# First experts of a two-block model: tokens scattered to their slots in DRAM instead of a one-hot dispatch on TensorE

## What is computed

```python
def grouped_experts(x, expert, gate, w_gate, w_up, w_down):
    # tokens sorted by expert, each expert's rows padded to whole chunks
    xs = jnp.concatenate([x, jnp.zeros((1, d), x.dtype)], axis=0)[slot_tok].reshape(n_blocks, DISPATCH_BLOCK, d)
    ...
    def run(args):
        xb, e = args
        return (jax.nn.silu(xb @ w_gate[e]) * (xb @ w_up[e])) @ w_down[e]

    ys = lax.map(run, (xs, block_e)).reshape(cap, d)
    return jnp.zeros((n + 1, d), x.dtype).at[slot_tok].add(ys * slot_w[:, None])[:n]
```

## Time and profile before

| | |
|---|---|
| median of 3 runs | 2183.39 us (2183.11 to 2185.64) |
| profiled execution | 2182.89 us, its span 2181.1 us |
| busy in the span | TensorE 86%, weight loads 61%, DVE 41%, ACT 30%, GpSimd 25% |
| moved by DMA | 574.35 MB, 263 GB/s over the span |
| experts of layer 0 | 48 chunks, 366 to 897 us |
| experts of layer 1 | 37 chunks, 1173 to 1632 us |

### The profile page before, as it was taken

The page is one execution under the profiler, slowest core; times in us unless marked ns, Lnnn a source line. Parts: engine busy times, 40 slices in busy tenths (PEclk is TensorE's granted clock), DMA queues, the critical chain, the costliest instruction groups (busy, mean ns, idle before and its releaser), DMA issues.

```text
span 2181.1 us, 56144 instructions
## 1 busy us (share of the span) xinstructions
PE 1882.8 (86%) x23126; PEld 1338.9 (61%) x23127; DVE 896.6 (41%) x2096; ACT 656.3 (30%) x1229; POOL 551.5 (25%) x407
## 2 busy tenths in 40 slices
PE   5999989979977999699977997666666988899998
PEld 3555457657655667364566765545545775678886
DVE  2087243545543555644624442222224993310001
ACT  1100243534532454521533442222224322120001
POOL 0000002656644666200102442222239001000000
PEclk9999999999988999799998998888887997899999
DMA  9778648999999886532024999999993352133320
GB/s 374 288 273 306 231 177 338 422 424 422 421 423 421 363 324 257 186 116 82 26 78 171 400 425 421 420 424 422 420 416 132 116 193 77 39 116 135 135 97 20
DMA packets 133060, 574.35 MB, mean 263 GB/s; under 512 B 4720, under 2 KB 9840, under 8 KB 116464
## 3 DMA queue, kind: packets, MB, share of 16 engines
q1 hardware_dynamic: 132688, 570.72, 66.2%
q10 hardware_dynamic: 288, 2.43, 0.3%
HBM read 572.08 MB, written 1.05 MB: 263 GB/s over the span
## 4 chain that ended last, share of the span: by engine, by line
PE 62%; DMA 23%; DVE 6%; ACT 4%; issue 3%; SPq 1%; DVEq 0%; ACTq 0%
PE bank L325 24%; DMA ring<-in_expert_w_gate 15%; PE bank L511 15%; DMA ring<-in_expert_w_up 6%; PE bank L467 5%; PE bank L488 4%; PE bank L854 3%; PE bank L558 2%; DVE b L894 2%; ACT b L1573 2%; PE bank L396 1%; PE bank L777 1%; DMA ring<-in_conv_w_in 1%; SPq L2014 1%; DMA ring<-in_ada_w 1%
## 5 line engine op out<-in xcount | busy, mean ns | idle before, releaser
L511 PE MATMUL bank<-ring,b 128*32 128x128 f32 (+1 forms) x13600 | 538.1, 313 | 150.3 <-issue 66.7
L511 PEld LDWEIGHTS bank<-ring,b 128*32 128x32 f32 x13600 | 413.2, 117 | 333.0 <-issue 222.6
L894 DVE TENSOR_TENSOR h_t<-h_t,bank 128x512 f32<-128x512 f32 (+1 forms) x696 | 350.7, 566 | 560.9 <-PE bank L488 560.9
L1573 ACT ACTIVATE b<-bank 128x128 f32<-128x128 f32 (+3 forms) x546 | 186.2, 366 | 1155.1 <-PE bank L467 411.8
L325 PE MATMUL bank<-h_t,ring 128*128 128x256 f32 (+1 forms) x1728 | 470.0, 433 | 8.6 <-DVE h_t L1359 3.6
L325 PEld LDWEIGHTS bank<-h_t,ring 128*128 128x128 f32 x1728 | 333.0, 194 | 131.6 <-issue 91.1
L1962 POOL TENSOR_SCALAR b<-b 128x1024 f32<-128x1024 f32 (+1 forms) x85 | 195.3, 2297 | 79.3 <-POOL b L1970 37.1
L1970 POOL TENSOR_TENSOR b<-b 128x512 f32<-128x512 f32 (+1 forms) x85 | 89.7, 1056 | 476.4 <-PE bank L488 476.4
L1573 ACT ACTIVATE b<-b 128x256 f32 (+5 forms) x186 | 181.7, 1021 | 27.9 <-DVE b L894 14.5
L488 PE MATMUL bank<-b 32*128 32x512 f32 (+1 forms) x1392 | 176.8, 580 | 5.5 <-DVE h_t L894 4.8
L1965 POOL TENSOR_TENSOR b<-b,b 128x1024 f32<-128x1024 f32 (+1 forms) x85 | 161.1, 1895 | 7.1
(11 more groups left out here) (238 smaller groups left out, 1461.5 us busy)
## 6 DMA issues: line engine op xcount, KB each, us to landing
ring<-in_expert_w_gate SPq DMA_DIRECT2D x64, 2048.0 KB, 22.3
ring<-in_expert_w_up SPq DMA_DIRECT2D x64, 2048.0 KB, 24.3
ring<-in_expert_w_down SPq DMA_DIRECT2D x64, 2048.0 KB, 25.6
ring<-in_ada_w SPq DMA_DIRECT2D x24, 2048.0 KB, 18.8
ring<-in_w_mod SPq DMA_DIRECT2D x12, 2048.0 KB, 13.7
ring<-in_w_in SPq DMA_DIRECT2D x6, 2048.0 KB, 12.0
ring<-in_conv_w_in SPq DMA_DIRECT2D x5, 2048.0 KB, 20.1
ring<-in_w_ffn_gate SPq DMA_DIRECT2D x5, 2048.0 KB, 7.7
```

The lines of the kernel that those rows point to most:

```text
L511: last = pe.matmul(b[32 * m:32 * m + 32, 0:width], lhs[:, k, :], rhs[:, k, m * width:(m + 1) * width], start=(k == 0), stop=(k == nk - 1), ...
L894: return dv.tensor_tensor(o, a, b, op)
L1573: return ac.activation(o, i, f, **kw)
```

## The change

The experts of layer 0 get their tokens by DMA (`by_dma`), those of layer 1 as before.

- A tensor `slot_rows` in DRAM has a row of 1024 channels for each slot, 2176 in all. ACT issues one DMA behind its part of the first modulation that fills it with zeros, from a zeroed stretch of SBUF. DVE waits for `zeroed` before the router.
- DVE casts the slot numbers to integers (`slot_i`). After `placed` GpSimd issues eight indirect DMAs, for four tiles of 128 tokens and both slots of a token, each of which writes 128 rows of 4 KB to their slots. Its four diagonals come behind them.
- ACT waits for all eight (`scattered`) and loads the 32 rows of chunk 0 as 128 rows of 256 channels (`load_rows`, 128 KB). TensorE turns them with two transposes (`turn_rows`), ACT copies them to `xe` (`take_rows`) and issues the next chunk's load. In the loop the transposes stand where the dispatch stood, and turn the rows of chunk n+1.
- Gone in layer 0: the one-hot table, all dispatches, `take_quarter`, `take_xe`, `take_h`.
- In both layers the channels of `h_tok` are put in another order, with ACT's copies writing with a stride of 128. The dispatches ahead of layer 1's loop then read contiguous weights, and so does its `take_h`.
- TensorE counts the chunks in a register of its own (`chunk_no`).

```diff
+ROWS = P * (-(-(MOST + 2) * CAP // P))
...
+        slot_rows = nc.dram_tensor("slot_rows", (ROWS, D), F32).ap()
+        quarter_rows = slot_rows.rearrange("s (m c) -> (s m) c", m=4)
+        zeros = b3[:, 4736:5248]
...
+                def turn_rows(b):
+                    transposes(b, [(P * i, x_rows[:, P * i:P * i + P]) for i in range(2)]).then_inc(s["xq_full"], 1)
+
+                if by_dma:
+                    pass
+                else:
+                    pe.wait_ge(s["disp_ready"], 8)
+                    for q in range(4):
+                        dispatch(bank[q], lambda t, kk: h_tok[:, t, (2 * q + kk) * P:(2 * q + kk + 1) * P], 0)
...
-                pe.wait_ge(s["xq_taken"], 4)
+                if by_dma:
+                    pe.wait_ge(sem("rows_loaded"), 16)
+                    turn_rows(bank[3])
+                else:
+                    pe.wait_ge(s["xq_taken"], 4)
...
+                            if by_dma:
+                                pe.wait_ge(sem("rows_loaded"), n * 16 + 32)
+                                turn_rows(bank[3])
...
+                if layer == 0:
+                    for j in range(2):
+                        step(dv.tensor_copy(slot_i[:, 4 * j:4 * j + 4], fl(g[j])))
+                    done()
...
+            dv.wait_ge(sem("zeroed"), 16)
             moe(0, 4)
...
-                    taken(act(h_tok[:, t, cols], b[:, :], ACT.Copy))
+                    rows = h_tok[:, t, :].rearrange("p (k q) -> p q k", k=KD)
+                    taken(act(rows[:, 64 * half:64 * half + 64, :], b.rearrange("p (q k) -> p q k", k=KD), ACT.Copy))
...
+                def load_rows(n):
+                    ac.dma_start(x_rows, quarter_rows[bass.ds(n * P, P), :]).then_inc(sem("rows_loaded"), 16)
+
+                def take_rows(n):
+                    ac.wait_ge(s["xq_full"], n + 1)
+                    act(xe.rearrange("p (m h) s -> p h s m", h=2), bank[3][:, 0:256].rearrange("p (h s m) -> p h s m", h=2, m=4),
+                        ACT.Copy).then_inc(s["xe_taken"], 1)
+                    load_rows(n + 1)
...
+                if by_dma:
+                    ac.wait_ge(sem("scattered"), 16 * 8)
+                    load_rows(0)
...
             modulate(0, 0, "h_a0")
+            ac.dma_start(slot_rows.rearrange("(p r) (h c) -> p (r h) c", p=P, c=512),
+                         zeros.unsqueeze(1).broadcast_to([P, 2 * ROWS // P, 512])).then_inc(sem("zeroed"), 16)
...
                 po.wait_ge(sem(f"placed{layer}"), 1)
+                if layer == 0:
+                    for t in range(tiles):
+                        for j in range(2):
+                            at = bass.IndirectOffsetOnAxis(slot_i[:, 4 * j + t:4 * j + t + 1], 0)
+                            po.indirect_dma_start(slot_rows, at, h_tok[:, t, :], None).then_inc(sem("scattered"), 16)
```

## The result

The changed kernel takes 2217.7 us (median of 4 runs, 2216.6 to 2220.8), the kernel before 2184.0 (2183.1 to 2185.6): ratio 1.016, 95% interval 1.014 to 1.017. The profiled execution has a span of 2215.2 us, 34.1 more than before. I forecast slower by 12, to at most 2217; the sign holds, the size doesn't.

The account below looks back on a forecast made before the run. Bounds by stage: TensorE work counts in 17 of 48 first expert chunks, added bytes in the other stages. Profiled 2182.9 us plus 14 + 4 + 11 - 13.6 - 3 = +12.4 gives 2195.3, said as 2196; range 2181 to 2217.

Parts of the forecast that it names:

- Fill, +14: Opening: the zero fill shares the full DMA engines with queued weights, so the second convolution chunk comes late; +14 us.
- Rival A: Opening: the fill is hidden, since writes to DRAM don't compete with loads; 2182, no change; chance 0.17 shared with another rival.
- Entry, +4: Before layer 0's experts: scatter and row load replace the dispatch, and the stretch bound by loads starts at 382.5; +4 us.
- the next weight load is issued by then: Entry: prefetch and first row load end some 382.5, with the next weight load already issued, so no idle DMAs.
- The 15.5 us of dispatch: Entry: removing the one-hot table and 64 dispatch matmuls gains nothing; first gate at 366 to 371, where 366.36 was.
- Row loads, +11: DMA-bound stretch of layer 0's experts: each of 30 chunks pays 0.37 us for its row load; +11 us.
- the 25th expert's weights: Sign in layer 0's expert loop: these weights come some 15 us later.
- Compute-bound chunks, -13.6: Last 17 chunks of layer 0: transposes replace dispatch instructions and save 0.8 us a chunk; -13.6 us.
- The wait for `hid`: Last 17 chunks: TensorE waits for DVE's `hid` before the hidden transpose, so 0.8 us a chunk is gained, not 1.5.
- Rival C: Last 17 chunks: rows come late and TensorE waits; 2226, or 2210 for half of that; chance 0.23.
- Layer 1, -3: Before the second experts: contiguous dispatch weights give -4, strided token copies ahead of the router cost +1; -3 us.

Follow-up runs that it names:

- e1: The changed kernel with the zero fill issued in `gated`, at its second channel block, and no longer in the opening: 2208.6 us.
- e5: The kernel before with the new channel order of the token rows alone, no fill, scatter or row loads: 2178.5 us, ratio 0.9971.
- e2: The changed kernel with SyncE waiting for the scatter before it issues the six prefetched expert weights: 2204.4 us.
- e3: The changed kernel with SyncE's wait for the scatter in front of the fourth of the six prefetched weights: 2212.2 us.
- e11: The changed kernel with SyncE holding the six prefetched weights until the first row load has landed: 2206.3 us.
- e6: The changed kernel with ACT copying landed rows into a second tile, from which TensorE turns them, packets unchanged: 2213.9 us.

## Why the prediction was wrong

**Fill, +14: right in kind, 11.7 measured.** One packet for one packet, as said, ACT not held. The convolution chunk came 10.3 late, and the matmuls behind it took 8.71 for 7.03, as the term had it from the earlier trace rows. The term was 2 us too high because the chunk was there at 90.4 and not at 92.5: both queues together moved 408 GB/s, not 386. That the start came out right was luck: the fill was issued at 40.62, not at 44.6, but its first packet stood at 44.8. e1's profiled execution gives the term back in full. Rival A falls.

**Entry, +4: the step that failed; 23.2 measured, outside its bounds.** The prediction had the rule, packets in turn, and the three sizes, and still took the scatter to be done at 352 to 362. It let the scatter run beside the 2 KB packets of the last piece. In the trace its first packet is at 356, 4.6 us behind the first issue, and only 41 of the 2 KB packets start after that; from there it stood against the 16 KB packets of gates and ups, and in between against the 4 KB packets of the first down. By the prediction's own rule the time was to be had: the scatter has 64 packets an engine; 32 of them pass beside the 32 of two gates and two ups, at 0.16 + 0.61 us, and 32 beside those of the first down, at 0.32, which is 24.6 + 10.2 = 34.8 us. It took from 356 to 392.4. Its first issue was 17 us later than the diagonals in the earlier trace rows, of which the fill is 11.7 and the copies most of the rest. Then the second half of the step fell too: it held that the engines would not idle because "the next weight load is issued by then". But the first gate, which frees the slot, stood behind scatter and row load, and the engines idled for 16 us (21 at a share of 0.23). The 15.5 us of dispatch were not gained, as the prediction had said, since scatter and row load took their place; in the kernel before they did count, for e5, with a shorter dispatch, has its first gate 3.65 us earlier and its span 4.0 shorter. e2 and e3 show the cause. By the profiled spans e2 gives back 12.5 of the 23.2, and e11, with both waits cured, no more. The 10.7 that stay are not taken apart by any run here: the scatter's 4.2 MB are 10 us at 420 GB/s wherever they stand, and the entry also begins later by the copies.

The Trainium skill (DMA: Bandwidth & Descriptors, Queues, rings and completion order) has the turn by packets, and the trace agrees, with 187 to 184. The estimate worked out from the same page of the Trainium skill (Anatomy of one DMA), eight scatters one behind the other in 25.6 us, does not hold: in e2 the eight were issued from 352.5 on, 1.26 apart, and all there at 368.6.

**Row loads, +11: right, 11.1.** The prediction proposed to read it at the 25th expert's weights, some 15 late where the entry alone makes 4. They are 46.0 late, 34.9 of it from ahead of the loop.

**Compute-bound chunks, -13.6: -11.4 measured.** The wait for `hid` is there, 0.50 us before the transpose, in 11 of 17. The 0.8 was near: with rows in time a chunk takes 8.99 (e6), 0.9 less than the 9.89 before. Rival C came in part: rows late in 7 chunks, 4 us. In these chunks a row load took 6.0 us in the median, less than the 6.8 that I had worked out for a window of 7.7, but anything from 2.0 to 10.0; one figure for all of them hid the late ones. (In the stretch bound by loads the median is 9.2.)

**Layer 1, -3: -0.7.** The dispatch took 5.72 and not 3.9. The row, 0.12 us a matmul, was taken at full clock; here, behind waits for VectorE of 5 us and more, the granted clock was 0.67 in the mean of 1199 to 1205 us, so for the greater part at the lower of its two levels, 1.2 GHz. With strided weights this could not be seen: a matmul took 0.24 at a mean clock of 0.89 in layer 0 and 0.25 at 0.62 in layer 1. At full clock, in layer 0 of e5, the gain is 8.1 us for 64. And the copies took 1.6 more, not 1, all of it in front of the router.

The sum of the terms as measured, 11.7 + 23.2 + 11.1 - 11.4 - 0.7, is 33.9; 19 of the 21.5 us by which I missed lie in the entry.

## To carry over

Before a small-packet transfer is put on a critical path, count its packets an engine and multiply by the packet time of whatever else is queued there then: its bytes alone don't tell. 4 MB that took 12 us with the weights held back (e2) took 36 beside their 16 KB and 4 KB packets. A prefetch that is early for its own consumer should be held back behind such a transfer, and bulk writes belong where the window of DMA shares has a gap. When a change has several parts, time each alone: the one that was meant as a by-product, kept alone, is faster than both kernels.

## What the runs showed of the hardware

- A load of 128 x 1 KB took 1.9 us from issue to landing alone and 9.2 in the median beside weight loads (10.7 at most); as 32 x 4 KB it took 6.6 beside them.
- Row loads that don't put one packet on each of 128 partitions slow the 16 KB packets beside them, from 0.617 us in the mean to 0.646 (4 KB on 32 partitions), 0.650 (2 KB on 64) and 0.647 (1 KB on 32). One packet in twenty took 0.84 us or more in the first, 0.79 in the second, 0.70 in the third; 0.63 in the changed kernel.
- Eight indirect DMAs of 128 rows by 4 KB are issued 1.26 us apart and overlap; the first packet came 4.6 us behind the first issue (3.7 in e2).
- A copy of 128x512 from PSUM with an eightfold stride in its output takes 0.9 us on ACT and on VectorE, against 0.5 contiguous on ACT.
- A 128x128 matmul with its weights at a stride of eight elements took 0.24 to 0.25 us at a mean granted clock of 0.89 and of 0.62; contiguous, 0.115 at full clock and 0.18 at 0.67.
